# Forget-gate sums formed once, joined weight loads, and re-timed hand-overs in a three-block decoder kernel

## The reference

```python
h = rms_norm(x, pre_g)
p = split_columns(h @ w_in + b_in)             # 14 groups of up to 512 columns
log_f = log_sigmoid(p["fox_f"] + forget_bias)  # 4 heads
cum = cumsum(log_f, axis=1)                    # forget-gate sums
z = q @ k.T * scale + cum[q] - cum[k]          # one of four kinds of attention
mix = concat(o_sb, o_nsa, o_fox, o_mla) * silu(gates)
x = x + rms_norm(mix @ w_out, post_g)
```

## Time and profile before

| what | value |
|---|---|
| median of 3 runs | 2084.08 us (2081.74 to 2085.05) |
| profiled execution, own time | 2084.3 us |
| its span, first to last instruction | 2082.7 us |
| PE busy | 2012.2 us, 97% of the span |
| DVE busy, ACT busy | 1123.3 us, 931.3 us |
| HBM read | 357.23 MB, 173 GB/s over the span |
| mean granted TensorE clock | 0.989 |

### The profile page before, as it was taken

One profiled execution on the slowest core, in us unless ns is written; L12 is line 12 of the kernel. 1 busy time (PEld: TensorE's weight loads), 2 busy tenths in 40 slices (PEclk: granted clock), 3 DMA queues, 4 the chain that ended last, 5 costly groups with the idle time before them and its releaser, 6 DMA issues.

```text
span 2082.7 us, 27966 instructions
## 1 busy us (share of the span) xinstructions
PE 2012.2 (97%) x10370; PEld 1712.6 (82%) x10370; DVE 1123.3 (54%) x1309; ACT 931.3 (45%) x1215; POOL 76.8 (4%) x126
## 2 busy tenths in 40 slices
PE   7999999998999999998999887999999999999998
PEld 6889988887789998887888766888888888888886
DVE  4474555555556464554647864644445544444443
ACT  5355434444454444444554434444444444433442
POOL 3000000001100000001100100000000000000000
PEclk9999999999999999999999999999999999999999
DMA  7584455665665444665545423566666666656553
GB/s 256 163 251 124 137 167 157 186 198 147 201 195 188 140 155 127 206 187 152 169 152 152 129 74 122 181 192 186 189 191 191 191 183 190 191 187 207 202 202 112
DMA packets 209513, 360.80 MB, mean 173 GB/s; under 512 B 22641, under 2 KB 45728, under 8 KB 209152
## 3 DMA queue, kind: packets, MB, share of 16 engines
q1 hardware_dynamic: 203728, 345.36, 54.3%
q0 software_dynamic: 4816, 13.76, 2.3%
q10 hardware_dynamic: 864, 0.27, 0.1%
HBM read 357.23 MB, written 2.10 MB: 173 GB/s over the span
## 4 chain that ended last, share of the span: by engine, by line
PE 90%; DVE 3%; ACT 2%; DMA 1%; issue 1%; SPq 1%; DVEq 1%; ACTq 0%; POOL 0%; POOLq 0%
PE psum L551 24%; PE psum L553 24%; PE psum L552 24%; PE psum L559 3%; PE psum L561 3%; PE psum L562 3%; DVE wl L522 1%; DMA raw<-in_w_in_dram 1%; SPq L506 1%; PE psum L627 1%; DVE conv_y L766 1%; PE psum L867 1%; PE psum L641 1%; PE psum L616 1%; ACT wh L515 1%
## 5 line engine op out<-in xcount | busy, mean ns | idle before, releaser
L522 DVE TENSOR_TENSOR wl<-raw,wh 128x1024 fp32r<-128x1024 f32 (+2 forms) x672 | 797.4, 1197 | 735.9 <-ACT wh L515 728.9
L515 ACT ACTIVATE wh<-raw 128x1024 fp32r<-128x1024 f32 (+2 forms) x672 | 690.5, 1036 | 879.4 <-PE psum L553 712.1
L551 PE MATMUL psum<-wh,xh 128*128 128x512 f32 (+2 forms) x1600 | 623.7, 390 | 1.2 <-DVE xl L809 1.2
L553 PE MATMUL psum<-wh,xl 128*128 128x512 f32 (+2 forms) x1600 | 616.7, 385 | 0.0
L552 PE MATMUL psum<-wl,xh 128*128 128x512 f32 (+2 forms) x1600 | 616.5, 385 | 0.0
L551 PEld LDWEIGHTS psum<-wh,xh 128*128 128x128 f32 x1600 | 302.3, 189 | 62.6 <-DVE xl L809 2.9
L553 PEld LDWEIGHTS psum<-wh,xl 128*128 128x128 f32 x1600 | 301.9, 189 | 59.5
L552 PEld LDWEIGHTS psum<-wl,xh 128*128 128x128 f32 x1600 | 302.6, 189 | 57.4
L551 PE MATMUL psum<-wh,mh 128*128 128x512 f32 x384 | 153.3, 399 | 18.0 <-issue 9.8
L553 PE MATMUL psum<-wh,ml 128*128 128x512 f32 x384 | 152.2, 396 | 0.0
L552 PE MATMUL psum<-wl,mh 128*128 128x512 f32 x384 | 152.0, 396 | 0.0
(11 more groups left out here) (342 smaller groups left out, 1509.7 us busy)
## 6 DMA issues: line engine op xcount, KB each, us to landing
raw<-in_w_in_dram SPq DMA_DIRECT2D x264, 512.0 KB, 4.3
raw<-in_w_out_dram SPq DMA_DIRECT2D x96, 512.0 KB, 3.7
raw<-in_w_gate_dram SPq DMA_DIRECT2D x88, 512.0 KB, 3.6
raw<-in_w_up_dram SPq DMA_DIRECT2D x88, 512.0 KB, 3.6
raw<-in_w_down_dram SPq DMA_DIRECT2D x80, 512.0 KB, 4.1
bias<-in_b_in_dram POOLq DMA_DIRECT2D x18, 256.0 KB, 4.0
raw<-in_w_in_dram SPq DMA_DIRECT2D x16, 268.0 KB, 2.8
raw<-in_nsa_cmp_w_k_dram SPq DMA_DIRECT2D x32, 128.0 KB, 2.3
```

The costliest lines, as they stand in the source:

```text
L515: act.activation(wh[:, n % SPLIT_SLOTS, 0:k, 0:unit.n], raw[:, n % RAW_SLOTS, 0:k, 0:unit.n], ACT.Copy).then_inc(hi_done, 1)
L522: dve.tensor_tensor(out=wl[:, n % SPLIT_SLOTS, 0:k, 0:unit.n], in0=raw[:, n % RAW_SLOTS, 0:k, 0:unit.n], in1=wh[:, n % SPLIT_SLOTS, 0:k, 0 ...
L551: pe.matmul(o, ah_[:, kt, tok], hi_w, start=first, stop=False)
L553: ins = pe.matmul(o, al_[:, kt, tok], hi_w, start=False, stop=last)
```

## The change

The forget-gate sums are formed once in a layer: DVE writes `fox_col` (the gate at columns 0, 32 and 64), PE forms the cumulative sums of both blocks in three fp32 products (`fox_sums`, in stage 8), DVE cuts them into three bfloat16 parts (`fox_parts`, `fox_lower_parts`), and `fox_all_scores` adds them by one bfloat16 product for each score tile. The count logarithms of attention `a` are cut into two rounded parts and added by six products of 512 columns in all instead of eight in fp32. The columns of `nsa_win_small` and the compression weights are joined into one array each before the launch, so that a unit is one DMA. Some constants move from ACT's queue to SP's, behind unit 7; POOL's constants wait for x; x is loaded later between the first units. At a layer's end three units of the next layer are split before the last mid, the last unit is multiplied token block by token block, the sum of three groups is formed ahead, and x is updated in halves. In the third block rows of `w_out_2` that are ready are multiplied for all four column groups before the late ones (with an addition into x for each half of a group: eight additions instead of four), taps move, and parts of some mids move by one slot.

```diff
 def output_slots_2():
...
+    slots = [early(0, 4, 5), early(1, 4, 5), early(0, 6, 7) + early(1, 6), early(1, 7), early(2, 4, 5, 6),
+             early(2, 7), early(3, 4), early(3, 5, 6, 7) + late(0, 0, 1), late(0, 2, 3) + late(1, 0, 1),
+             late(1, 2, 3), late(2, 0, 1, 2, 3), late(3, 0, 1), late(3, 2, 3)]
+    slots[7][3].after_mid = 22
+    slots[8][0].after = "conv_rows2"
+    slots[8][2].after_mid = 23
...
+            if unit.by_rows:
+                for tb in range(TB):
...
+                    ins.then_inc(s("first_rows") if tb == 0 else unit_used, 1)
...
             update(0)
+            operand(0)
+            operand(1)
             update(1)
+            split(3)
+            last_group()
+            operand(2)
+            operand(3)
+            update(2)
...
-                for b in {0: (0, 1), 2: (2,), 5: (3,)}.get(n, ()):
+                for b in {0: (0,), 1: (1,), 3: (2,), 5: (3,)}.get(n, ()):
...
-                        if l == 0 and n < BLOCKS:
-                            load_x(n)
+                        if l == 0 and n in (0, 2, 3, 4):
+                            load_x(max(n - 1, 0))
                         load_unit(sp, place, n, unit, layer_src(l))
+                        if l == 0 and n == PARTS - 1:
+                            for dst, name in CONSTS[POOL_CONSTS:]:
+                                sp.dma_start(dst, d[name]).then_inc(consts_loaded, 16)
...
-                pool_rstd(place.once, "post", [(slice(0, TB), DM)])
+                pool.wait_ge(s("post_sums"), place.once)
+                stand_alone(pool, "pool")
+                pool.tensor_tensor(out=rstd[:, 0:TB], in0=sq_sums[:, 0:TB], in1=minus_half.to_broadcast([P, TB]),
+                                   op=ALU.pow).then_inc(s("post_rstd"), 1)
...
                 def fox_all_scores():
                     for h, blk, o, n, opens in score_places():
-                        sp0 = fox_sp[:, h:h + 1].to_broadcast([P, P])
-                        sp1 = fox_sp[:, 4 + h:5 + h].to_broadcast([P, P])
                         pe.matmul(o, fox_qT[:, h, blk * P:(blk + 1) * P], fox_kT[:, h, 0:n], start=opens, stop=False,
                                   skip_group_check=True)
-                        pe.matmul(o[:, 0:P], sp0, tri_up[:, :], start=False, stop=False, skip_group_check=True)
-                        if blk:
-                            pe.matmul(o[:, P:T], sp0, one.to_broadcast([P, P]), start=False, stop=False,
-                                      skip_group_check=True)
-                            pe.matmul(o[:, P:T], sp1, tri_up[:, :], start=False, stop=False, skip_group_check=True)
+
+                    for h, blk, o, n, _ in score_places():
+                        pe.matmul(o, fox_pick[:, h:h + 1].to_broadcast([P, P]), fox_rows[:, 0:n], start=False,
+                                  stop=False, skip_group_check=True)
...
+            def a_masks():
+                for part in (count_hi, count_lo):
+                    for bank, m, table in ((0, 2, part[:, 0:T]), (1, 2, part[:, 0:T]), (2, 4, part[:, T:T + P])):
+                        o = st[:, bank * 512:(bank + 1) * 512].rearrange("p (m c) -> p m c", m=m)
+                        ins = pe.matmul(o, ident_r[:, :], over(table, m), start=False, stop=True,
+                                        skip_group_check=True)
...
-            taps_at_unit = {first_tap_unit + SLOT_UNITS * i + n: 1 for i, m in enumerate((4, 4, 3, 3, 3)) for n in range(m)}
-            taps_at_mid = {9: 2, 15: 3, 16: 4, 17: 2, 18: 3}
+            taps_at_unit = {first_tap_unit + SLOT_UNITS * i + n: 1 for i, m in enumerate((4, 2, 3, 3, 3)) for n in range(m)}
+            taps_at_unit.update({first_tap_unit + 5 * SLOT_UNITS + n: 1 for n in range(4)})
+            taps_at_mid = {9: 2, 15: 1, 16: 4, 18: 5}
...
-                1: first_queries, 3: kv_group,
+                1: first_queries, 2: lambda: head_scale("cq02", 0, 512, split_heads(cqn)), 3: kv_group,
...
-                11: lambda: (head_sums("aq2", 512), sinks_max("c10", 8), head_scale("aq2", 1, 512, split_heads(aqn)), sinks_sum("c10")),
-                12: lambda: (dve_copy_half(probT2)),
+                11: lambda: (sinks_max("c10", 8), head_sums("aq2", 512), sinks_sum("c10")),
+                12: lambda: head_scale("aq2", 1, 512, split_heads(aqn)),
...
```

More of the change, by code:

```diff
@@ L63 @@
 OPERAND_ALIGN = 2048
+SMALL_COLUMNS = ((3072, 268), (5388, 4), (6416, 64))
+N_SMALL = sum(w for _, w in SMALL_COLUMNS)
 GROUPS = (
@@ L134, in output_slots, with early, late @@
     units[6].after_mid = NG * 2
+    units[-1].by_rows = True
     return slots_of(units)
 def output_slots_2():
[L141 to L150 removed]
+    def early(g, *pairs):
+        return [output_unit("w_out_2", g, pair, 7, 4) for pair in pairs]
+    def late(g, *pairs):
+        return [output_unit("w_out_2", g, pair, 3, 0) for pair in pairs]
+    slots = [early(0, 4, 5), early(1, 4, 5), early(0, 6, 7) + early(1, 6), early(1, 7), early(2, 4, 5, 6),
[4 more added lines that the diff above has]
+    slots[8][2].after_mid = 23
+    return slots
 CMP_SLOTS = (6, 7)
@@ L162 @@
 UNITS_2 = sum(len(s) for s in SLOTS_2)
+CONV_UNIT = sum(len(s) for s in SLOTS_2[:WIN_SLOTS_2 + 8]) + 1
 FFN_STEPS = DFF // GN
@@ L1095, in nsa_compress_hidden, with fox_sums @@
                                             skip_group_check=True)
+                    return ins
+                def fox_sums():
+                    o = st[:, 1280:1280 + T]
+                    for first, which, table in ((True, 0, tri_up[:, :]), (True, 0, None), (False, 1, tri_up[:, :])):
+                        dst = o[:, 0:P] if table is not None and first else o[:, P:T]
+                        ins = pe.matmul(dst, fox_col[:, which, :], one.to_broadcast([P, P]) if table is None else table,
+                                        start=first, stop=True, skip_group_check=True)
                     return ins
```

263 lines of the change are left out of this document (175 added, 88 removed).

## The result

The changed kernel took 2054.45 us (median of 4 runs, 2050.74 to 2057.2) against 2084.57 us for the kernel before in the same rounds: a ratio of 0.9856, interval 0.9838 to 0.9875. So 30 us were won where I forecast 43.6. The time lies 6.5 us above the forecast's own range (2033 to 2048) and 1.4 us above the wider one (2029 to 2053), to which I had given 8 in 10. The profiled execution is the fastest of the four, 2050.74 us with a span of 2049.1. Five further runs of it lie between 2050.2 and 2055.9 us.

The account below looks back on a forecast made before the run. PE was taken as the bound, busy 2012.2 of 2082.7 us, with idle time and half-speed clock to win. Terms summed to 43.6 us off 2084.3, giving 2041 us; own range 2033 to 2048, wider 2029 to 2053 at 8 in 10.

Parts of the forecast that it names:

- Start: Before the first product: one x block moves behind later weights and fewer loads compete; gain 1.3 us, bounds nothing and 3.5.
- Joined loads: Slots 6 and 7 of both layers: two SP issues a pair in place of seven; gain 8.5 of 8.9 us idle.
- Layer ends: Both layer ends: earlier first product and a shorter slow-clock stretch; gain 2.8 and 1.5, together 4.3 us, bounds 2.3 and 8.
- Forget sums: Forget-gate sums in each layer: sixteen fp32 products replaced by three and eight bf16 ones; gain 2.1 us a layer, 4.2.
- Slot 2 of block 3: Third block, slot 2: mid 1 loses POOL's power and the scaling; idle and slow clock go, gain 3.8 us, bound 2.3.
- Slot 12: Third block, slot 12: mid 11 ready 4.7 us earlier, 1.0 us of wait stays; gain 5.1 us, bounds 3 and 7.
- Slots 16 to 28 with count logarithms: Third block's last section: 7.5 us less waiting, clock loss 8.5 to 2, gain 14.0; logarithms' cheaper products add 2.4 us.
- lower bound of 3.7 us: Gain in slots 6 and 7 of both layers if the load rate stays at 234 GB/s, in place of 8.5 us.
- two clock terms: Layer ends (4.3 us) and third-block slots 16 to 28 (14.0 us), both counting on less half-speed time after shorter waits.
- DVE holding the third block: Rival, 17%: third-block waits only move because DVE's work holds them; its gains fall to 4 and 3 us, 2053 us.
- The clock staying up: Rival, 17%: waits under 3 us leave PE at 2.4 GHz; last section gains 22, layer ends 8: 2029 us.
- Joined rows that bring less: Rival, 10%: joined rows in slots 6 and 7 move no faster; gain 3.7 in place of 8.5 us, 2045.5 us.

Follow-up runs that it names:

- run 3: Changed kernel with the loads of slots 6 and 7 issued in the old pieces again, from the same joined arrays: 2055.9 us, ratio 0.9857 to the kernel before.
- run 9: The changed kernel itself, timed and profiled a second time with nothing altered: 2054.0 us, ratio 0.9853 to the kernel before.
- run 10: Changed kernel with the old pieces of the loads in slots 6 and 7, a second turn of run 3: 2055.5 us, ratio 0.9866.
- run 12: Kernel before with the joined arrays alone, one issue per compression or narrow unit in place of four or three: 2082.7 us, ratio 0.9989.
- run 13: Changed kernel whose compression units load only half their columns, splits and products the same: 2045.7 us, ratio 0.9822.
- run 14: Changed kernel in which ACT and DVE split only half the columns of compression units, loads and products the same: 2042.9 us, ratio 0.9802.
- run 7: Changed kernel with unread filling products at layer ends and in the third block, and the narrow group's bias in one load: 2042.4 us, ratio 0.98.
- run 6: Changed kernel with three convolution taps moved into DVE's waits in mids 17 and 19, same work: 2045.5 us, ratio 0.9817.
- run 4: Changed kernel with the narrow group's three broadcast bias loads made one in both layers: 2051.3 us, ratio 0.9839.
- run 11: Changed kernel with run 6's taps, one bias load, and filling products at layer ends, slot 20 and before the convolution's rows: 2036.5 us, ratio 0.9776.

## Why the prediction was wrong

The direction, the bound, and most places were right; the sum was 13.5 us too large. By its own steps, in us, predicted and measured. The measured ones make 31.2 with 2.0 for the joined loads; the medians differ by 30.1, the two profiled executions by 33.6. All rows are from the first profiles but that of the joined loads, which goes by medians; in the first profiles slots 6 to 8 differ by more than that, which is most of what the rows lack to 33.6.

| Step | predicted | measured | from |
|---|---|---|---|
| Start | 1.3 | 1.7 | first product at 12.05 and 10.38 |
| Joined loads | 8.5 | 1.4 to 2.3 | runs 3, 9, 10, 12 |
| Slot 2 of the layers | 0 | 2.1 | waits 1.3 and 1.3; 0.4 and none |
| Layer ends | 4.3 | 1.3 | to the 48th product |
| Forget sums | 4.2 | 3.6 | stage 21 6.6 and 3.7, twice; less 1.3 for products and 0.9 for waits in stage 8 |
| Slot 2 of block 3 | 3.8 | 4.0 | windows: 2.3 us idle gone, clock 0.91 to 1.00 |
| Slot 12 | 5.1 | 5.6 | wait 5.75 and 0.8; clock 0.83 to 1.00 |
| Slots 16 to 28 with count logarithms | 16.4 | 10.9 | last product of the second layer to the end: 1103.2 and 1083.0, less 4.0 and 5.6, and 0.3 lost at that layer end added |

**The step that failed first is the joined loads.** Of SP's seven issues a pair I wrote "That is why PE waits 4.9 and 4.0 us." The issues are gone in the changed kernel and in run 12, and most of the waiting is not (9.0 us idle before, 5.5 and 6.5 in the changed kernel's two profiles, 6.9 in run 12). SP's 3.59 us from unit to unit are issuing indeed (seven times 0.48 are 3.4), but that was only part of the picture. These are the views of SP's waits of the kernel before, 98 to 128 us, and of the changed kernel, 98 to 130 us (us in total, times, longest); a load waits there for the buffer that DVE's split has to release:

```profile
SPq L497 <- DVE wl L522: 9.1, 6, 2.9
```

```profile
SPq L513 <- DVE wl L538: 21.6, 16, 4.4
```

What the issues no longer take, SP now waits for buffers, and runs 13 and 14 show the loop through landing and both splits as what holds these slots. So the failed term is the gain of 8.5 us, which measured 1.4 to 2.3, and the failed step is that only issues and bytes were priced and never the time for which a buffer is away. My lower bound of 3.7 us rested on the window's rate, a bytes argument; it lies above what was measured, though inside run 12's interval. Of the Trainium skill's page "DMA: Bandwidth & Descriptors", section "Specifications", whose 512 B I weighed there: in run 12, whose only change is longer rows and fewer issues, the two windows went from 236 to 229 and from 216 to 225 GB/s, so longer rows brought no rate worth the name. Run 14 moved more than the changed kernel with the same rows (271 against 252). So the rate in these slots follows when loads are issued, and no run here tests the page's figure.

**The step that failed next is the clock**, put as "with no wait over 3.5 us the clock's loss falls from 8.5 to 2", and for the layer ends as a fall that shrinks with the wait. The waits came out nearly as walked through: 11.3 us idle from 1180 to 1311, 12.5 forecast; the largest ahead of slots 18 and 24, as forecast; 3.0 and 1.05 at a layer end. But waits of 2.2 to 4.2 us still brought three stretches at 1.2 GHz in the last section, 17.0 us long in all (10.2 in run 9) where the kernel before has 20.4, and one of 6.8 us at each layer end, where the kernel before has 6.8 and 3.4. At a layer end the first product did come 3.0 us earlier, 3.7 forecast; the clock and the second block's transposes took half of that back at the first end and all of it at the second. PEclk behind slot 16 is 0.90, where I wanted above 0.95.

By the table the two clock terms fell short by 3.0 and 5.5 us and the joined loads by 6 to 7, while the other rows came out 2.6 us better than forecast. Filling gave 4.1 and 6.3 us back, more than the 8.5 that the clock terms lacked, because the sum had allowed for some loss in both. So run 7 landing within 2 us of the forecast is luck: products that nobody reads and one bias load made up there for a term of the joined loads that stays missing.

**The forget sums** were off by a wait: DVE's column sums at the end of mid 7 are now what the rope transposes wait for. Slot 2 of the layers I had at nothing; the norm's chain ends earlier against PE's program there, and why was not tried.

**The rivals.** DVE holding the third block (2053 us) was nearest in number and wrong as a cause: the section idles 11.3 us and not 18, and run 6 took the waits away without taking work off DVE. The clock staying up (2029 us) did not happen. Joined rows that bring less was right in its direction, for another reason than mine.

**The start** needs one more remark: two blocks of x had to come before, now one, and the gain is one transfer as forecast.

## What to carry to other kernels

A queue that issues slowly ahead of a wait need not be its cause: look whether the issuing engine itself waits for a free buffer, and count the whole loop (landing, every pass over the data, next issue) against the buffers in the ring. A wait of TensorE that has been made shorter is not yet cheaper in proportion: waits of 2.2 to 4.2 us here mostly cost their length and a stretch at half clock, as those of 5.75 us did before. Ask whether the work behind it was waiting anyway; where it was not, put products that nobody reads into the wait, or move work of the engine it waits for into that engine's own idle time, which won 9 us here where filling won 5. Where runs of one kernel differ by 3 us, no single trace sizes a 2 us term; profile the same kernel twice before you read a difference off two traces. And a total that lands on the forecast proves no term of it.

## What the runs showed of the hardware

- The same waits bring different clocks. Runs 3 and 10 are one kernel; a wait of 2.2 us at slot 20 and one of 2.8 us at slot 24 are each followed by a stretch at 1.2 GHz (6.8 and 3.4 us) in run 3 and by none in run 10, and the third block is 4.0 us shorter. Runs 13 and 14 are like run 10 there (1214 to 1234 us in run 13 reads 1.00, in the changed kernel 0.83), and the changed kernel's waits of 3.3 and 3.0 us in slot 6 were not followed by one either. Length alone does not decide; what does stays open.
- Products of 128 by 128 in fp32 on a constant tile, 18 of them in a hand-over of 6 us, keep the clock at 1.00; in the kernel before 30 of them cost nothing either (ratio 1.0001).
- Three broadcast loads of 268, 4 and 64 columns of bias, made one, went with a shorter wait of PE for weights from another queue: 1.4 us in run 4 and 1.5 in run 11 against 3.3 and 3.0 in the changed kernel's two profiles, but 2.6 in run 7.
